# Router-gate scatters of two token tiles interleaved, first head of each written without add; scan-time modulation weights multiplied in five blocks

## The reference, cut to what matters

```python
def adaln(cond, w, b):
    m = jax.nn.silu(cond) @ w + b
    return jnp.split(m[:, None, :], 6, axis=-1)
...
def block(x):                       # PEER, one tile of 128 tokens
    q = (x @ w_q).reshape(n, P_HEADS, 2, P_QDIM // 2)
    s = jnp.einsum('nhjd,hjkd->nhjk', q, sub_keys).astype(jnp.float32)
    sv, si = lax.top_k(s, P_TOPK)
...
    tv, ti = lax.top_k(cand, P_TOPK)
    eidx = jnp.take_along_axis(cidx, ti, axis=-1)
    gate = jax.nn.softmax(tv, axis=-1).astype(x.dtype)
    u = u_tab[eidx]
    act = jax.nn.gelu(jnp.einsum('nhkd,nd->nhk', u, x), approximate=False)
    return jnp.einsum('nhk,nhkd->nd', gate * act, v_tab[eidx])
```

## Time and profile before

| | us |
|---|---|
| median of 3 runs | 2975.25 |
| lowest and highest | 2974.61, 2990.54 |
| profiled execution | 2986.64 |
| its span | 2984.7 |
| PE busy / DVE busy / ACT busy / POOL busy | 2857.3 / 1953.9 / 1027.6 / 997.6 |
| mean granted TensorE clock, as a share | 0.984 |

### The profile page before, as it was taken

How to read it: one execution, slowest core, us unless ns; L and a number is a source line. 1 busy time by engine, 2 the same in 40 slices (tenths; PEclk the granted TensorE clock), 3 DMA queues, 4 the chain that set the end, 5 groups by cost and what they waited for, 6 DMA issues and landing times.

```text
span 2984.7 us, 47694 instructions
## 1 busy us (share of the span) xinstructions
PE 2857.3 (96%) x18222; PEld 2513.0 (84%) x18222; DVE 1953.9 (65%) x4284; ACT 1027.6 (34%) x1428; POOL 997.6 (33%) x695
## 2 busy tenths in 40 slices
PE   7989999999999999999999979999999969999998
PEld 4965558999999998888888868999999967888886
DVE  3775654588862237888886475587772214888887
ACT  4611104333453332222224264333453322222222
POOL 0000000137777742233310000126787771242430
PEclk9999999999999999999999989999999989999999
DMA  6346624777787788989973313677687758898984
GB/s 237 112 148 226 227 93 148 287 186 175 176 228 175 175 233 275 316 302 317 309 268 118 106 43 120 245 219 174 165 226 188 175 114 274 290 313 307 314 298 161
DMA packets 345559, 631.63 MB, mean 212 GB/s; under 512 B 79184, under 2 KB 226768, under 8 KB 343072
## 3 DMA queue, kind: packets, MB, share of 16 engines
q1 hardware_dynamic: 140960, 428.57, 44.1%
q0 software_dynamic: 86400, 99.92, 14.0%
q10 hardware_dynamic: 118016, 100.67, 10.6%
HBM read 533.37 MB, written 95.35 MB: 211 GB/s over the span
## 4 chain that ended last, share of the span: by engine, by line
PE 59%; POOL 21%; DMA 8%; issue 5%; DVE 5%; ACT 1%; ACTq 0%; SPq 0%; DVEq 0%; POOLq 0%
PE ps L1215 32%; POOL g_dram L2509 14%; POOL g_dram L2503 6%; DMA g_dram<-arena 5%; PE ps L611 5%; PE ps L613 5%; PE ps L612 5%; DMA ring<-in_ada 2%; DVE arena L1654 2%; PE ps L584 1%; PE ps L721 1%; PE ps L672 1%; PE ps L1162 1%; PE ps L703 1%; PE ps L788 1%
## 5 line engine op out<-in xcount | busy, mean ns | idle before, releaser
L1654 DVE TENSOR_TENSOR w_lo<-ring,w_hi 128x1024 fp32r<-128x1024 f32 x576 | 701.9, 1221 | 530.4 <-ACT w_hi L1304 526.6
L611 PE MATMUL ps<-hT_hi,w_hi 128*128 128x384 f32 x2576 | 867.8, 337 | 28.7 <-ACT arena L1580 28.5
L612 PE MATMUL ps<-hT_lo,w_hi 128*128 128x384 f32 x2576 | 861.4, 334 | 0.0
L1215 PE MATMUL ps<-w_hi,ga_parts 128*128 128x512 f32 x2560 | 846.8, 395 | 1.8 <-DVE ga_parts L1654 1.8
L613 PE MATMUL ps<-hT_hi,w_lo 128*128 128x384 f32 x2384 | 797.3, 334 | 0.0
L1304 ACT ACTIVATE w_hi<-ring 128x1024 fp32r<-128x1024 f32 x378 | 400.0, 1060 | 972.9 <-PE ps L613 773.7
L1215 PE MATMUL ps<-w_lo,ga_parts 128*128 128x512 f32 x1536 | 606.0, 395 | 0.0
L1215 PEld LDWEIGHTS ps<-w_hi,ga_parts 128*128 128x128 f32 x2560 | 482.3, 188 | 115.4 <-issue 3.1
L611 PEld LDWEIGHTS ps<-hT_hi,w_hi 128*128 128x128 f32 x2576 | 484.3, 188 | 32.6 <-issue 32.1
L2509 POOL DMA_INDIRECT g_dram<-arena x256 | 459.9, 1797 | 146.7 <-issue 88.8
L612 PEld LDWEIGHTS ps<-hT_lo,w_hi 128*128 128x128 f32 x2576 | 484.3, 188 | 0.5
(11 more groups left out here) (337 smaller groups left out, 2310.4 us busy)
## 6 DMA issues: line engine op xcount, KB each, us to landing
ring<-in_u SPq DMA_DIRECT2D x256, 512.0 KB
ring<-in_v SPq DMA_DIRECT2D x256, 512.0 KB
ring<-in_ada SPq DMA_DIRECT2D x96, 512.0 KB
act_dram<-arena SPq DMA_DIRECT2D x256, 192.0 KB
arena<-g_dram ACTq DMA_DIRECT2D x32, 1280.0 KB
arena<-act_dram ACTq DMA_DIRECT2D x32, 1280.0 KB
g_dram<-arena POOLq DMA_DIRECT2D x24, 1024.0 KB, 23.6
ring<-in_mix_in SPq DMA_DIRECT2D x42, 512.0 KB
```

The lines of the kernel that those rows point to most:

```text
L611: pe.matmul(out, hi[:, c, :], hT_hi[:, c, :], start=(c == 0), stop=False)
L612: pe.matmul(out, hi[:, c, :], hT_lo[:, c, :], start=False, stop=False)
L1215: mm = pe.matmul(ps[:, 2 * t + nb, :], l_, r_[:, cs], start=(first and q == 0), stop=(last and q == len(pairs) - 1), skip_group_check=True)
L1654: return dve.tensor_tensor(out, a, b, op)
```

## The change

The two token tiles' scatters get a semaphore each (`scattered[0]`, `scattered[1]`), and their heads are issued in turn: h0 to h4, w0, h5, w1, h6, w2, h7, w3, then w4 to w7. A head waits only for the head before it of its own tile, w0 only for VectorE's ranking of tile 1 (`scatter_ready`). The 8 DMAs of h0 and the 16 of w0 are plain writes, without add. ScalarE waits for both semaphores; the wait ahead of `fin_g` is for tile 1's alone. In the scan the 16 modulation tiles of a unit are multiplied in blocks of 3, 3, 3, 3 and 4 at (2, 0), (3, 0), (4, 0), (5, 0) and (6, 0), where before eight pairs stood at s = 0 and s = 2 of levels 2 to 5.

```diff
@@ -52,6 +52,8 @@
 UNITS = [(0, 0), (1, 0), (0, 1), (1, 2), (0, 2), (1, 1)]
 
 
+ADA_AT = [(2, 0), (3, 0), (4, 0), (5, 0), (6, 0)]
+ADA_RUNS = [3, 3, 3, 3, 4]
 MIX_OUT0 = [(0, 2), (0, 3), (1, 2), (1, 3), (0, 0), (0, 1), (1, 0), (1, 1)]
 MIX_OUT1 = [(nb, q) for nb in range(2) for q in range(4)]
 ROWS_MIX = [[(0, 0), (1, 0), (0, 1), (0, 2), (1, 1), (1, 2)], [(nb, t) for nb in range(2) for t in range(3)]]
@@ -416,7 +418,7 @@
         zeros_ready = sem("zeros_ready")
         g_zeroed = sem("g_zeroed")
         scatter_ready = sem("scatter_ready")
-        scattered = sem("scattered")
+        scattered = [sem(f"scattered{t}") for t in range(2)]
         chosen_moved = sem("chosen_moved")
         act_gathered = sem("act_gathered")
         v_gathered = [sem(f"v_gathered{i}") for i in range(VSLOTS)]
@@ -572,11 +574,11 @@
                 pe.wait_ge(landed[g % RING], 16 * (g // RING + 1) + it * 16)
                 return ring[:, g % RING, :].rearrange("p (c n) -> p c n", c=DC)
 
-            def ada_pair(G, j):
-
-                if j == 0 and G:
+            def ada_tiles(G, first, count):
+
+                if first == 0 and G:
                     pe.wait_ge(ada_row_ready, G)
-                for i in (2 * j, 2 * j + 1):
+                for i in range(first, first + count):
                     b, w = i // 4, tile_landed(ada_group_at(G), i).rearrange("p c n -> p (c n)")
                     for cc in range(2):
                         c = 2 * (i % 4) + cc
@@ -1029,8 +1031,9 @@
                             products(q + 1, GAM, RHO)
                         if s == 2 and 2 <= lv < 5:
                             row(q + 1, lv - 2)
-                        if s != 1 and 2 <= lv < 6:
-                            ada_pair(q + 1, 2 * (lv - 2) + s // 2)
+                        if at in ADA_AT:
+                            j = ADA_AT.index(at)
+                            ada_tiles(q + 1, sum(ADA_RUNS[:j]), ADA_RUNS[j])
 
                 pe.wait_ge(proj_taken, 26)
                 pe.wait_ge(knorm_root, NF)
@@ -1266,8 +1269,7 @@
                 at = stage_tiles(layer)
                 if layer == 0:
                     pe.wait_ge(silu_ready, 1)
-                    for j in range(8):
-                        ada_pair(0, j)
+                    ada_tiles(0, 0, 16)
                     ada_columns(0)
                 norm_T(2 * layer)
                 if layer == 0:
@@ -1584,7 +1586,8 @@
                             act.activation(tv, tv, ACT.Exp).then_inc(gexp_ready, 1)
                     if k in (NJ - 8, NJ - 4):
                         b = int(k == NJ - 4)
-                        act.wait_ge(scattered, 16 * (GATHERED + P) * (layer + 1))
+                        act.wait_ge(scattered[0], 16 * GATHERED * (layer + 1))
+                        act.wait_ge(scattered[1], 16 * P * (layer + 1))
                         for i in range(2):
                             act.wait_ge(g_stored[i], 16 * 4 * SPREAD * (layer + 1))
                         for i in range(ASLOTS):
@@ -2494,20 +2497,41 @@
                     pool.dma_start(to_scatter[kp], chosen_of[GATHERED:P, 0:2, c]).then_inc(chosen_moved, 16)
                     pool.dma_start(to_gather[kp], chosen_of[0:GATHERED, :, c]).then_inc(chosen_moved, 16)
                 pool.wait_ge(chosen_moved, 64 * (layer + 1))
-                done = (GATHERED + P) * layer
-                for h in range(NH):
-                    if h:
-                        pool.wait_ge(scattered, 16 * (done + 8 * h))
+
+                def half_tile(h):
+
                     for k in range(8):
+                        if h and k == 0:
+                            pool.wait_ge(scattered[0], 16 * (GATHERED * layer + 8 * h))
                         c = NH * k + h
-                        pool.indirect_dma_start(g_flat, bass.IndirectOffsetOnAxis(to_scatter[:, 1, c:c + 1].bitcast(U32), 0), to_scatter[:, 0, c:c + 1],
-                                                None, compute_op=ALU.add).then_inc(scattered, 16)
-                pool.wait_ge(scatter_ready, 2 * layer + 2)
-                for h in range(NH):
-                    pool.wait_ge(scattered, 16 * (done + GATHERED + TOPK * h))
+                        at, gate = to_scatter[:, 1, c:c + 1].bitcast(U32), to_scatter[:, 0, c:c + 1]
+                        if h == 0:
+                            ins = pool.indirect_dma_start(g_flat, bass.IndirectOffsetOnAxis(at, 0), gate, None)
+                        else:
+                            ins = pool.indirect_dma_start(g_flat, bass.IndirectOffsetOnAxis(at, 0), gate, None, compute_op=ALU.add)
+                        ins.then_inc(scattered[0], 16)
+
+                def whole_tile(h):
+
+                    if h == 0:
+                        pool.wait_ge(scatter_ready, 2 * layer + 2)
                     for k in range(TOPK):
-                        pool.indirect_dma_start(g_flat, bass.IndirectOffsetOnAxis(whole_at[:, k, h:h + 1], 0), whole_gate[:, k, h:h + 1], None,
-                                                compute_op=ALU.add).then_inc(scattered, 16)
+                        if h and k == 0:
+                            pool.wait_ge(scattered[1], 16 * (P * layer + TOPK * h))
+                        at, gate = whole_at[:, k, h:h + 1], whole_gate[:, k, h:h + 1]
+                        if h == 0:
+                            ins = pool.indirect_dma_start(g_flat, bass.IndirectOffsetOnAxis(at, 0), gate, None)
+                        else:
+                            ins = pool.indirect_dma_start(g_flat, bass.IndirectOffsetOnAxis(at, 0), gate, None, compute_op=ALU.add)
+                        ins.then_inc(scattered[1], 16)
+
+                for h in range(5):
+                    half_tile(h)
+                for h in range(3):
+                    whole_tile(h)
+                    half_tile(5 + h)
+                for h in range(3, NH):
+                    whole_tile(h)
 
             def gather_rows(layer):
 
@@ -2542,7 +2566,7 @@
             pool.dma_start(skT, A["keys"][1]).then_inc(keys_in, 16)
             scatter_gates(1)
             pool.wait_ge(selT_taken, 2 * SPREAD)
-            pool.wait_ge(scattered, 2 * 16 * (GATHERED + P))
+            pool.wait_ge(scattered[1], 2 * 16 * P)
             pool.dma_start(fin_g, A["final_norm"].partition_broadcast(P)).then_inc(fin_in, 16)
             gather_rows(1)
 
```

## The result

| | before | after |
|---|---|---|
| median, 10 runs each | 2978.14 us | 2960.88 us |
| lowest and highest | 2969.7, 2995.62 | 2954.75, 2970.64 |
| ratio | | 0.9932 [0.991, 0.9954] |
| profiled execution, its span | 2986.64, 2984.7 | 2954.79, 2953.0 |
| mean granted clock | 0.984 | 0.988 |

What follows compares the result with a forecast made beforehand. GpSimd's scatter chain bounds the end of layer 1's U stage, TensorE everything else there. Stall -28.0, slow clock -2.2, layer 0 -0.5, scan -6.9 make -37.6 us: 2975.25 to 2938 us, range 2926 to 2957.

Steps and rivals of the forecast that it cites:

- the target: End of layer 1's U stage: the last scatter must land 28.0 us earlier to cost TensorE nothing.
- The term of the sum for the stall, -28.0: TensorE's idle time at the end of layer 1's U stage goes whole: -28.0 us.
- the -2.2 for the slow clock: After layer 1's stall TensorE runs 8 us at 0.73 mean granted clock; without the stall, -2.2 us.
- The seven waits: GpSimd's waits for landings ahead of h5 to h7 and w0 to w3 go: -28.4 us on layer 1's chain.
- A: Plain writes are no cheaper than added ones; 3.2 us of layer 1's stall stay, time 2941; chance 0.22.
- D: The DMA queue paces the scatters; waits return at h1 to h4 and w4 to w7, time 2968; chance 0.07.
- E: Slower: a plain 4-byte scatter costs GpSimd more than an added one; 2990 at 1.47 us above; chance 0.03.
- I carry the difference over: Whole kernel: the profiled execution's forecast gain of 37.6 us is taken off the median, 2975.25, which gives 2938 us.
- Rival C: Executions without profile have a shorter stall, which is the 11.4 us; only 26 us to gain, 2949; chance 0.12.
- the scan's -6.9: Modulation blocks in the scan: waits -26.1, added array time +9.7, waits and delays left +9.5, sum -6.9 us.
- under 12 as the sign of being right: Waits for modulation tiles in the scan sum to under 12 us with five blocks a unit.
- Rival B: The scan gives nothing: blocks wait as pairs did and pay extra array time, -30.7 + 9.7, 2954; chance 0.12.

Runs made afterwards that it cites:

- x2: The changed kernel with the scan's eight pairs of before instead of five blocks, so the scatter part alone: 2955.65 us, ratio to before 0.9935.
- x4: The changed kernel with pairs and plain writes, but the heads in the old order: 2956.0 us, ratio to before 0.9923.
- y1: The changed kernel again, unaltered, on the second batch's chip: 2951.25 us, ratio to before 0.9861.
- y2: The changed kernel without its plain writes, so turns and five blocks alone: 2951.1 us, ratio to before 0.9861.
- z1: Kernel with turns, added scatters and pairs, loading a quarter of each modulation tile of the scan (results not the reference's): 2938.86 us, ratio to before 0.9804.
- z3: The changed kernel with pairs and every scatter an addition, base of the third batch: 2955.24 us, ratio to before 0.986.
- q1: The changed kernel with pairs spread over levels 1 to 6 and no plain writes: 2941.36 us, ratio to before 0.9829.
- q3: The changed kernel with pairs spread over levels 1 to 6 and only h0's writes plain: 2940.81 us, ratio to before 0.9821.
- r1: The changed kernel with pairs spread over levels 1 to 6 and only w0's writes plain: 2937.26 us, ratio to before 0.9845.
- r2: As r1, with a wait for the landing after every fourth write of w0: 2941.0 us, ratio to before 0.9857.
- y3: The kernel before once more, unaltered, for a second trace of its stalls: 2999.5 us, ratio to before 1.0013.
- x1: The kernel before with the five modulation blocks alone, scatters as they were: 2975.99 us, ratio to before 0.9986.
- first batch: Runs x1 to x4 on one chip, beside the kernel before, which took 2974.27 us there.
- z2: As z1, with the quarter-size loads, but five blocks instead of pairs: 2941.93 us, ratio to before 0.9815.
- p1: The changed kernel with the scan's tiles in eight pairs spread over levels 1 to 6, plain writes kept: 2960.28 us, ratio to before 0.987.
- q2: p1 again, spread pairs with all plain writes, on the fourth batch's chip: 2951.93 us, ratio to before 0.9858.
- q4: The changed kernel again, unaltered, on the fourth batch's chip: 2964.81 us, ratio to before 0.9899.
- first, second and fifth batch: One chip each: x1 to x4, then y1 to y4, then r1 and r2; the kernel before took 2974.27, 2994.18 and 2983.35 us.
- third and fourth batch: One chip each: z1 to z3 with p1, then q1 to q4; the kernel before took 2998.82 and 2995.07 us.
- y4: The kernel before, old order and pairs, with only h0's 8 scatters made plain writes: 2964.1 us, ratio to before 0.9903.
- x3: The changed kernel with pairs and no plain write, so turns alone: 2955.37 us, ratio to before 0.9924.

## Why the prediction was wrong

**Right: the path and the target.** The chain of scatters bounded the end of layer 1's U stage and nothing else in it was near. Off it, a U stage takes 569 us in twelve traces (x2 to x4, y1, y2, z1 to z3, q1, q3, r1 and r2: 568.8 to 570.1), all with turns or with all plain writes and without a standstill. The term of the sum for the stall, -28.0, and the -2.2 for the slow clock come to 30 us, which is what y1 to y3 show between 598.9 and 569.3.

**Right: the steps on the chain.** The seven waits went (0.30 us in their place), plain writes take 0.96 us against the forecast 0.945, and w0 did not come too early. The chain from first to last scatter got 70 us shorter in layer 1 (469 to 399) where I had 39: the waits fell by 43 us (67.3 to 24.4) instead of 28.4, and the scatters' own time by 30 (349.2 to 319.6) instead of 10.7. Rivals A, D and E fall: plain writes are cheaper, no wait of over 5 us stands at w4 to w7, and nothing is slower. That GpSimd's scatters stretch beside VectorE, for which the prediction cited the Trainium skill ("SBUF — State Buffer", shared port pair), shows again: in the trace after, 33 added scatters with VectorE all but idle beside them take 1.55 us on average, the other 309 take 1.78. It did not matter, as the slack is 50 us.

**Wrong, step 1: "I carry the difference over."** The sum was made against a profiled execution 11.4 us above the median, and took its whole stall for the median's. Rival C had this. The traces of the old order of additions lose 0.5 and 30 us in their two U stages (before), 12 and 15 (x1), 12 and 30 (y3, where layer 1's 28 us recur, on a chip whose median is 16 us higher), while a kernel without that chain on the path has 569 us twice. Take this loss off the profiled time and 2956.3, 2953.0 and 2957.4 us are left. So the first chip's median of 2978.14 would have some 22 us of stall and not 30: an estimate, as no trace of an execution at the median was kept. On the chip of the first batch the stall is worth 18 to 19 us in the medians (x2 to x4), not 30.7. The kernel before has medians of 2974, 2978, 2983, 2994, 2995 and 2999 us in its six timings, and in one of them its executions spread over 40 us even without the longest; x2 to x4 spread over 8 to 15. Against 2975.25 step 1 takes the 11.4 us off the gain, which gives C's 2949.

**Wrong, step 2: the scan's -6.9.** The sum took the ring's waits of 26.1 us off and put 9.5 back for what my walk through unit 1 left; the measured remainder is 22.4 (17.6 and 4.8 in the lines above), where I had named under 12 as the sign of being right. I let a buffer count as loaded in time because its place was later. But the ring's transfers are the bound there (z1), and three tiles at one place ask for them in a burst: waits stay, and the third tile pays besides (z2). Pairs spread over more places, with the same bytes, have waits of 5.2 and 6.5 us (p1, q1). The scan stage takes 285.7 us with full blocks (mean of five traces, 280.3 to 290.1) and 288.1 with pairs (seven traces, 286.1 to 291.0). So the blocks gain some 2.4 us, with more scatter than that, and x1's ratio can't tell it from nothing. Rival B had this mechanism, with too high a price for the array time (9.7; z2 less z1 has 4.2). This step is about 4.5 us.

**Wrong, step 3: no rival for it.** The plain writes have a price on GpSimd's issue, -14.4 us, and none anywhere else: I put their effect on the rest of the kernel at nothing, without a reason. Seven traces have both bursts. Four of them, on three chips (the changed kernel's first, p1, q2 and q4), have standstills at the end of w0's burst; three, on two other chips (x2, x4 and y1), have none. They cost 7.6 us in the profiled execution of the changed kernel and 10.6 in the medians of q2 against q1. This fits with the changed kernel taking 2961 and 2965 us where its trace shows standstills and 2951 where it shows none.

Together: 2938 + 11.4 (step 1) + 4.5 (step 2) + 7.6 (step 3) = 2961.5; measured are 2960.88. The sizes are from single executions, and the median before went from 2975.25 to 2978.14 with more of them, so part of this agreement is luck.

**Not settled.** What holds TensorE's count back. It is shown that on one chip taking the plain writes of w0 away takes the standstills away (q1 to q4), and that on two others they stay out with the same writes (x2, x4, y1). Whether it is their kind, their pace, or both bursts together was asked by r1 and r2 and got no answer. The chips also differ in their traces. The increments that DMAs give to semaphores are all but complete on the chips of the first, second and fifth batch, 27,873 to 27,929 of 27,984 in every trace, and short by a fifth on the chip of the first timing and in the third and fourth batch, 21,979 to 22,998. The page shows it by the time from issue to landing, which it gives for complete records only, here after and then x2:

```profile
ring<-in_u SPq DMA_DIRECT2D x256, 512.0 KB
```
```profile
ring<-in_u SPq DMA_DIRECT2D x256, 512.0 KB, 4.0
```

Standstills at w0's burst stand in the short traces alone: in all four of them that have both bursts, in none of the six that lack w0's (before, z1 to z3, q1, q3). So it takes the plain writes and something else, which goes with the loss of records. Whether that is the chip or the recording itself, and whether the standstill would be there without a recording, no run shows. One thing that the counts show: the software queue has 81024 packets where before had 86400, so the 48 plain writes need 112 fewer each, 16 in place of 128 (y4, with 16 of them, has 84608, again 112 fewer each). The Trainium skill ("DMA: Bandwidth & Descriptors", Queues, rings and completion order) says that an engine drains a whole packet of one queue before it turns to the next; longer packets would hold others longer by it, but no run here shows that eight elements of 4 bytes hold anything for 8 us. A single standstill of 5.37 us with the same unknown releaser in layer 1's V stage, in the changed kernel and in q3, has no plain write near it.

**The better kernel.** Spread pairs with plain writes of h0 alone or none (q3, q1) take 2941 us, 23.5 us less than the changed kernel on the same chip. r1 has 2937 on its own, but has not been tried where standstills occur.

## What to carry to other kernels

A stall that hangs on a chain of many small transfers has a length of its own in every execution and on every chip: forecast from the floor that the stage reaches without it, not from one trace's stall, and don't carry a profiled execution's excess over to the median if the stall may be what the excess is. Once one of two edits has taken a chain off the path the second buys nothing there, and may still cost something elsewhere: here turns alone gave the whole gain, and the plain writes brought a risk of 10 us. Where a wait hangs on several semaphores and the profile names no releaser, look in the code for all of them before you blame the transfer, and look whether the trace is complete. Where a ring of buffers paces a stage, spread its consumers evenly; to gather them at fewer places does not make the transfers faster.

## What was not expected of the hardware

- A write-only indirect DMA of 128 elements of 4 bytes occupies GpSimd 0.95 to 0.96 us at the shortest, one that adds 1.54, and the first makes 16 packets, the second 128.
- TensorE's increment of a semaphore can be recorded 8 to 10 us after the product that makes it, with the waiting engine starting 0.11 us behind the increment (8.3 us in the changed kernel, 10.0 in p1, 9.1 in q4, 8.6 in q2; 0.01 to 0.02 us in ordinary flow). These cases stand at a burst of 16 plain indirect writes and in traces that lack a fifth of their DMA increments. TensorE then stood for 5.31 us in the changed kernel, and over the 16 us around it 0.79 of the clock was granted.
- Two runs of one kernel with turns and without plain writes differ by 0.1 us between two chips (x3 2955.37, z3 2955.24), where the kernel before, with a chain of 192 small scatters as its bound, differs by 25 us between the same two (2974.27, 2998.82).
